# The opening of a transformer kernel: first modulation, first norm and the latents' products put into one block, and two later orders changed

## The reference, cut to what matters

```python
mod = silu(c) @ w_ada + b_ada                      # six sections of D: shift1, scale1, gate1, ...
h = rms_norm(x, norm1_g) * (1 + scale1) + shift1
z = h @ w_in                                       # 1024 x (256, 256, 64, 512, 512, 512)
c_q, c_kv, k_pe, dq, dk, dv = split(z)
q  = rms_norm(c_q, q_a_norm_g) @ w_q_up            # "latents": c_q and c_kv
kv = rms_norm(c_kv, kv_a_norm_g) @ w_kv_up
k_pe, dq, dk = rope(...)
lam = exp(sum(lambda_q1*lambda_k1)) - exp(sum(lambda_q2*lambda_k2)) + 0.2
d_out = norm((softmax(q1 k1) - lam * softmax(q2 k2)) v)
x = x + gate1 * (concat(mla_out, d_out) @ w_out)
h2 = rms_norm(x, norm2_g) * (1 + scale2) + shift2
for each block of 128 rows of one expert (32 experts, top 1 group of 4, top 2 of 8):
    y = (silu(xb @ w_gate[e]) * (xb @ w_up[e])) @ w_down[e]    # D_EXPERT = 512
x = rms_norm(x + gate2 * moe, final_norm_g)
# second block: rms_norm, modulate, conv mixer (three products D x D, ...), gated FFN
```

## Time and profile before

| | before |
|---|---|
| median of 3 runs (lowest, highest) | 2682.98 us (2680.89, 2684.83) |
| the profiled execution: its own time | 2683.05 us |
| its span | 2681.3 us |
| mean granted TensorE clock | 0.945 |
| PE busy | 2384.5 us (89%), 10764 matmuls |
| DVE busy | 1738.9 us (65%) |
| ACT busy | 1216.7 us (45%) |
| moved | 485.28 MB, mean 181 GB/s |

### The profile page before, as it was taken

How to read it: one execution, slowest core, us unless ns; L and a number is a source line. 1 busy time by engine, 2 the same in 40 slices (tenths; PEclk the granted TensorE clock), 3 DMA queues, 4 the chain that set the end, 5 groups by cost and what they waited for, 6 DMA issues and landing times. The chain is left out here.

```text
span 2681.3 us, 31591 instructions
## 1 busy us (share of the span) xinstructions
PE 2384.5 (89%) x10764; PEld 1908.4 (71%) x10764; DVE 1738.9 (65%) x1997; ACT 1216.7 (45%) x1623; POOL 450.7 (17%) x396
## 2 busy tenths in 40 slices
PE   2889996799798399999999759999899999999998
PEld 2667775477567288787777547887677888888886
DVE  5368886466495589999999665444338666653344
ACT  2236675366531277677676461110464333332332
POOL 0000000787500011000000110000004323220100
PEclk9899997899898599999999869999999999999999
DMA  5131121337655499999999863331532323245453
GB/s 207 44 118 36 48 70 39 105 97 244 231 180 194 146 390 398 398 399 398 397 399 397 300 227 104 109 110 56 172 91 67 94 70 89 75 121 185 146 171 115
DMA packets 268905, 485.28 MB, mean 181 GB/s; under 512 B 19410, under 2 KB 129423, under 8 KB 268303
## 3 DMA queue, kind: packets, MB, share of 16 engines
q1 hardware_dynamic: 235568, 364.37, 39.4%
q0 software_dynamic: 26912, 98.62, 11.1%
q10 hardware_dynamic: 6336, 21.11, 2.0%
HBM read 402.24 MB, written 76.55 MB: 179 GB/s over the span
## 5 line engine op out<-in xcount | busy, mean ns | idle before, releaser
L2059 DVE TENSOR_TENSOR e_w<-e_raw,e_w 128x1024 fp32r<-128x1024 f32 x384 | 442.2, 1217 | 60.2 <-ACT e_w L2123 59.7
L2123 ACT ACTIVATE e_w<-e_raw 128x1024 fp32r<-128x1024 f32 x384 | 376.6, 1050 | 191.4 <-PE e_pgu L255 148.1
L255 PE MATMUL e_pgu<-e_w,e_xt 128*128 128x512 f32 x1536 | 369.0, 397 | 16.5 <-DVE e_xt L2067 10.2
L255 PEld LDWEIGHTS e_pgu<-e_w,e_xt 128*128 128x128 f32 x1536 | 286.0, 189 | 91.1 <-DVE e_w L2059 17.8
L255 PE MATMUL s_ps<-h,s_w 128*128 128x512 f32 x1152 | 267.0, 394 | 5.4 <-DVE h L2459 5.4
L255 PEld LDWEIGHTS s_ps<-h,s_w 128*128 128x128 f32 x1152 | 218.9, 190 | 52.2 <-DVE h L2459 5.9
L255 PE MATMUL w_ps<-w_out,w_ring 128*128 128x512 f32 x1056 | 244.1, 390 | 2.2 <-DVE w_ring L3094 2.2
L255 PE MATMUL w_ps<-y 128*128 128x512 f32 x1056 | 240.2, 389 | 1.4 <-DVE w_o_full L3259 1.0
L255 PEld LDWEIGHTS w_ps<-w_out,w_ring 128*128 128x128 f32 x1056 | 198.1, 188 | 45.1 <-DVE w_out L3101 3.0
L255 PEld LDWEIGHTS w_ps<-y 128*128 128x128 f32 x1056 | 198.0, 188 | 43.4 <-issue 1.4
L255 PE MATMUL w_ps<-y,w_ring 128*128 128x512 f32 x816 | 195.9, 398 | 4.3 <-ACT w_h L2891 3.0
(11 more groups left out here) (388 smaller groups left out, 3882.5 us busy)
## 6 DMA issues: line engine op xcount, KB each, us to landing
e_raw<-in_w_expert_gate_dram SPq DMA_DIRECT2D x128, 512.0 KB, 6.7
e_raw<-in_w_expert_up_dram SPq DMA_DIRECT2D x128, 512.0 KB, 6.9
e_raw<-in_w_expert_down_dram SPq DMA_DIRECT2D x128, 512.0 KB, 7.1
w_raw<-in_ffn_w_gate_up_dram SPq DMA_DIRECT2D x48, 512.0 KB, 6.0
w_o_full<-in_ffn_w_down_dram SPq DMA_DIRECT2D x44, 512.0 KB, 4.0
y_rows<-am_zrow SPq DMA_DIRECT2D x4, 4352.0 KB, 34.3
raw_rows<-in_w_ada_dram POOLq DMA_DIRECT2D x32, 512.0 KB, 4.0
y_rows<-e_yo ACTq DMA_DIRECT2D x32, 512.0 KB, 6.3
```

Of the source, the lines that this page charges most:

```text
L255: o = pe.matmul(out, stat[i], mov[j], start=start and n == 0, stop=stop and n == 2)
L2059: dve.tensor_tensor(w[1][:, slot % CUT], raw[:, slot], w[0][:, slot % CUT].bitcast(F32), ALU.subtract).then_inc(low, 1)
L2123: act.activation(w[0][:, slot % CUT], raw[:, slot], ACT.Copy).then_inc(high, 1)
```

## The change

1. `load_constants`, `first_modulation` and `norm_transposed` are gone. Their work stands at the head of `diff_attention`'s block. x comes first, in eight pieces, then section 0 and section 1 of w_ada in eight pieces each through one set of eight slots. Each block of 128 rows of x is squared, scaled (now by ACT, out of `x_rows`) and turned as it comes; four of the turned blocks are copied out of PSUM by DVE (`copy_x`), four by ACT. DVE adds the sections (`add_section`) in between, the modulation is added up into columns, and `modulate(k)` (DVE, in place on `m_full`) makes h's chunk k, which is split at once.
2. The four latents are no longer made one after another. `latents()` takes the chunks k of depth in turn and does 24 matmuls for each, into eight PSUM banks, so that it begins with the first chunk of h and of the weights. The shared key (`LAT` is now 1 for the numbering of chunks) follows, with the sums of squares between its halves. The splits of weights, roots, inverses and norms behind it are written in another order.
3. In the experts' opening the row block's split stands behind two weight pieces.
4. In the combine stage SP issues the final norm's gain and then waits for the first gathered rows before it issues the conv's weights; the splits of the weights stand behind the first blocks' work, `columns` behind `scaled(3)`, `norm(3)` and two inverses ahead of it, two adds (4 and 5) and their squares behind `split(0)`.

DVE's queue from its first rows, before. `m_acc` is the sum over a section, `n_stage` the normed rows, `n_rstd` the inverse roots.

The diff, cut to its core:

```diff
-def load_constants(nc, g, a):
...
-def first_modulation(nc, g, a, room):
...
-def norm_transposed(nc, g, tag, gain, mod, out_t=None, split=None, ahead=None):
...
-    LAT = 5
+    LAT = 1
...
+        sec = nc.alloc_sbuf_tensor_at("m_sec", [P, KD, D], F32, offset=h_at[0])
+        acc = nc.alloc_sbuf_tensor_at("m_acc", [P, 2, D], F32, offset=e0_at)
...
+        lat_w = [nc.alloc_sbuf_tensor_at(f"m_lat_w{j}", [P, KD, 4 * P], F32R, offset=g.lat_at[j]) for j in range(2)]
...
+                for n in range(NT):
+                    sp.dma_start(x_rows[:, n, :], x_v[n]).then_inc(x_in[n], 16)
+                for t in range(KD):
+                    sp.dma_start(sec[:, t, :], sec_v[:, t, 0:D]).then_inc(sec_in[t], 16)
...
+                for t in range(KD):
+                    sp.wait_ge(part, t + 1)
+                    sp.dma_start(sec[:, t, :], sec_v[:, t, D:2 * D]).then_inc(sec_in[t], 16)
+                sp.dma_start(lat_raw_w[:], win[:, :, 0:4 * P]).then_inc(lat_w_in, 16)
...
+                def latents():
...
+                    for k in range(KD):
+                        pe.wait_ge(lw_low, k + 1)
+                        pe.wait_ge(h_low, k + 1)
+                        for c in range(4):
+                            for hf in range(2):
+                                to = (ps[:, c, halves[hf]] if c < 2 else pss[:, halves[hf]] if c == 2 else (pj, po)[hf][:])
+                                o = three_passes(pe, to, [v[:, k, c * P:(c + 1) * P] for v in lat_w], [v[:, k, halves[hf]] for v in h_t],
+                                                 k == 0, k == KD - 1)
+                            if k == KD - 1:
+                                o.then_inc(lproj, 1)
...
-                for c in range(LAT):
-                    latent(c)
+                pe.wait_ge(ident_in, 16)
+                for n in range(NT):
+                    turn_x(n)
+                    if n == 4:
+                        pe.wait_ge(rows_in, 16 * 9)
+                        for q in range(2):
+                            o = pe.transpose(rows_t[:, q, :], vrow[:, q, :], g.ident[:])
+                        o.then_inc(rows_turned, 1)
+                section(0)
+                section(1)
+                latents()
+                shared_latent()
+                pe.wait_ge(lat_raw, 4)
...
+                    act.activation(full[:, :, n * P:(n + 1) * P], ps[:, n % 2, :].rearrange("p (k q) -> p k q", q=P), ACT.Copy).then_inc(x_copied, 1)
...
+                square(0)
+                for n in range(NT):
+                    if n < NT - 1:
+                        square(n + 1)
+                    scale_x(n)
+                    if n >= 5:
+                        copy_x(n - 1)
+                copy_x(NT - 1)
...
+                act.wait_ge(lat_w_in, 16)
+                for k in range(KD):
+                    act.activation(lat_w[0][:, k, :], lat_raw_w[:, k, :], ACT.Copy).then_inc(lw_high, 1)
+                    act.wait_ge(affine, k + 1)
+                    act.activation(h_t[0][:, k, :], full[:, k, :], ACT.Copy).then_inc(h_high, 1)
                 w_leading(0, 0)
                 w_leading(0, 1)
-                w_leading(1, 0)
-                for c in range(4):
...
-                    w_leading(c + 1, 1)
-                    act.activation(lraw[:, c, :], ps[:, c % 2, :], ACT.Copy).then_inc(lat_raw, 1)
...
-                    act.activation(lsq[:, c, :], lraw[:, c, :], ACT.Square).then_inc(squared, 1)
-                    if c == 2:
-                        latent_root(0)
-                    if c < 3:
-                        w_leading(c + 2, 0)
...
+                latent_evict(0)
+                latent_evict(1)
+                latent_square(0)
+                latent_square(1)
+                latent_evict(2)
+                latent_evict(3)
+                latent_square(2)
+                latent_square(3)
+                w_leading(LAT, 0)
+                latent_root(0)
+                w_leading(LAT, 1)
+                latent_root(1)
                 latent_leading(0)
-                latent_root(1)
-                w_leading(LAT, 0)
-                w_leading(LAT, 1)
                 for c in range(3):
...
+                def copy_x(n):
...
+                    dve.tensor_copy(full[:, :, n * P:(n + 1) * P], ps[:, n % 2, :].rearrange("p (k q) -> p k q", q=P)).then_inc(x_copied, 1)
...
+                def modulate(k):
+                    dve.tensor_scalar(full[:, k, :], full[:, k, :], g.a_col[:, k:k + 1], g.mod[:, 0, k:k + 1], ALU.mult, ALU.add).then_inc(affine, 1)
...
+                inverse(0)
+                inverse(1)
+                copy_x(0)
+                inverse(2)
+                copy_x(1)
+                add_section(0)
+                inverse(3)
+                copy_x(2)
+                add_section(1)
+                inverse(4)
+                copy_x(3)
+                for t in range(2, 5):
+                    add_section(t)
+                    inverse(t + 3)
...
+                for t in range(5, KD):
+                    add_section(t)
+                dve.wait_ge(rows_turned, 1)
+                dve.tensor_copy(g.vcol[:], rows_t).then_inc(vec_ready, 1)
+                for t in range(KD, 2 * KD):
+                    add_section(t)
...
+                dve.tensor_tensor(g.mod[:, 0, :], pcol, g.col["first_b"], ALU.add).then_inc(mod_ready, 1)
...
+                dve.scalar_tensor_tensor(out=g.a_col[:], in0=g.mod[:, 0, 8:16], scalar=1.0, in1=g.col["norm1_g"], op0=ALU.add, op1=ALU.mult).then_inc(mod_ready, 1)
...
+                modulate(0)
+                for k in range(KD):
+                    lat_w_rest(k)
+                    if k < KD - 1:
+                        modulate(k + 1)
+                    h_rest(k)
...
+                w_rest(0)
+                w_rest_part(LAT, 0)
                 latent_inverse(0, 0)
+                w_rest_part(LAT, 1)
                 latent_inverse(0, 1)
-                w_rest_part(4, 0)
                 latent_norm(0, "q_g")
-                w_rest_part(4, 1)
+                latent_inverse(1, 0)
                 latent_rest(0)
-                w_rest_part(LAT, 0)
-                latent_inverse(1, 0)
-                w_rest_part(LAT, 1)
+                w_rest_part(LAT + 1, 0)
                 latent_inverse(1, 1)
+                w_rest_part(LAT + 1, 1)
                 latent_norm(1, "kv_g")
-                w_rest_part(LAT + 1, 0)
-                w_rest_part(LAT + 1, 1)
                 latent_rest(1)
...
-                rest_gu(0, range(CUT))
+                rest_gu(0, (0, 1))
                 x_rest(0)
-                rest_gu(0, range(CUT, 8))
+                rest_gu(0, range(2, 8))
...
+                sp.dma_start(fg[:], a["final_norm_g"].partition_broadcast(P)).then_inc(fg_in, 16)
+                sp.wait_ge(rows_in[0], 32)
                 for j, s in enumerate(order):
                     sp.dma_start(raw[:, j], w_v[:, :, s, 0:P]).then_inc(raw_in[j], 16)
-                sp.dma_start(fg[:], a["final_norm_g"].partition_broadcast(P)).then_inc(fg_in, 16)
-                sp.wait_ge(rows_in[0], 32)
...
-                for j in range(3):
-                    rest(0, j)
                 add(0)
                 add(1)
                 norm(0)
...
                 add(3)
                 norm(2)
                 inverse(1)
+                norm(3)
+                inverse(2)
+                rest(0, 0)
+                inverse(3)
+                rest(0, 1)
                 dve.wait_ge(col_out, 1)
                 dve.scalar_tensor_tensor(out=g.a_col[:], in0=g.mod2[:, 0, 8:16], scalar=1.0, in1=g.col["g0"], op0=ALU.add, op1=ALU.mult)
                 dve.tensor_copy(g.b_col[:], g.mod2[:, 0, 0:8]).then_inc(ab, 1)
-                norm(3)
-                inverse(2)
+                split(0)
+                rest(0, 2)
                 add(4)
-                inverse(3)
                 add(5)
-                split(0)
```

374 lines of the change are left out of this document (158 added, 216 removed).

## The result

| | before | changed |
|---|---|---|
| median of 4 runs (lowest, highest) | 2682.41 us (2680.89, 2684.83) | 2647.28 us (2646.87, 2647.80) |
| span of the profiled execution | 2681.34 us | 2645.66 us |

A forecast was written before the change was run, and what follows sets the result against it. PE, busy 89% of the span, was taken as the bound, with gains where it idles or waits. 2683.05 - 32.2 (opening, latents) - 5.4 (experts' start) - 0 (combine's start) = 2645.4 us; range 2634 to 2658.

The forecast's parts named there:

- A: Opening and latents up to the first scores: scores at 162.9 instead of 195.14, a gain of 32.2 us.
- B: Experts' start: x's split behind two weight pieces, not six, gains 5.4 us; bounds 0 and -5.6.
- C: Combine stage's start: earlier first add, given back by late acc and deferred adds, total 0; bounds -8 and +4.
- first root's end: Latents: ACT's first root, queued behind a weights' split that waits for PE, ends at 112.7; before, at 128.8.
- the start at the low clock: Latents' first products: PE's start at the low clock level adds 3 us to the 43.5 of 192 products.
- The rival of a slower DVE: Opening: copies cost 2.46 and modulates 1.28, first product 4.9 + 1.0 later, total 2651.3 to 2653; chance 0.17.
- w_in's load: Opening: w_in's 2 MB land at 42, hidden behind DVE's section adds.
- the room as some 9: Experts: a piece asked for 18.45 us ahead, less 6.8 landing and 2.3 split, leaves some 9 to spare.
- The rival in which the loads set the pace: Experts: loads set the pace after all, so the earlier start gains 0, total 2650.8; chance 0.08.
- the two things that give it back: Combine: acc lands by 1566, so columns at about 1573; two adds (5.2) and squares (3.1) deferred behind the split.
- the landing near 1558: Combine: by the skill's page small rows get a larger share, acc lands by about 1558, the stage gains 7.
- the rival of a low clock: Latents: PE fed by chunks stays at the low clock, each of 240 products 0.227 longer, total 2697; chance 0.03.

The follow-up runs named there:

- copies_act: The changed kernel, but all eight turned blocks of x are copied by ACT, none by DVE: 2643.98 us, ratio 0.9856.
- whole_h: The changed kernel, but PE begins the latents' products only when all eight chunks of h and of the weights are split: 2662.12 us, ratio 0.9924.
- root_first: The changed kernel, but the first latent root precedes the next weights' leading part on ACT, and its inverse that chunk's rest on DVE: 2642.74 us, ratio 0.9855.
- load_after: The changed kernel with one more 2 MB transfer, read by nobody, on SP's queue ahead of the experts' loop: 2652.02 us, ratio 0.9883.
- adds_early: The changed kernel, but the combine stage's adds 4 and 5 and their squares stand ahead of the wait for columns: 2644.26 us, ratio 0.9858.
- acc_first: The changed kernel, but the two stored sections are issued ahead of the conv's weights, whose second and third splits stand behind affine and split: 2640.69 us, ratio 0.9845.

## Why the prediction was right

The steps came mostly as laid out. That the total lies within 1.9 owes something to luck: A fell short by 1.0, B and C gave 0.7 and 0.4 more, and the stretches that the change does not touch added 2.0, which nobody forecast.

- **The opening.** Its steps, forecast and found: last section add 43.7 and 45.0; first product 51.4 and 52.49; last of 192 products 97.9 and 98.0; first root's end 112.7 and 112.92; scores 162.9 and 163.86. The agreement at 98.0 is two errors that cancel: the first product came 1.1 late, and the products took 45.6 and not 46.5, as the start at the low clock cost 2.0 and not 3. That DVE bounds the front was tested by taking its copies away (copies_act, -3.9), that PE sets the pace behind it by withholding the chunks (whole_h, +17.1 for 16.4 of delay), and that DVE's chain bounds most of the rest by moving the root (root_first, -3.0 for 4.3).
- **Mis-sized there.** DVE's section adds ended 1.3 late, because its copies and inverses reached it later than I laid out (the last root was out at 29.5 and not at 28.0; section 0's last add ended at 34.3, not 33.2, with the copy of the columns only behind it), and because the seven adds of section 1 took 1.37 each and not 1.31. Copy and modulate cost 1.23 and 0.81, where I took 1.21 and 0.75. The rival of a slower DVE did not come.
- **w_in's load** landed at 45.5, not at 42: I had the sections' last pieces arriving without a gap, but two of them waited for DVE's adds. It did not show in the time, as the modulation came later still; the cover was 3 us and not 6.
- **B.** -5.7 at the first product and -6.1 at the last split, where I took -5.4; undoing it alone cost 5.6 in the stage. The reason given, PE setting the pace because ACT hardly waits for landings, was half of the truth. The transfers stand level with PE: with 116 us of PE's work gone they still ran at 399 GB/s, and the stage was 1.7 shorter. What let PE gain 5.7 was the lead of at least 5.1 that each piece had. I counted the room as some 9, of which 5.6 go; the closest pieces had 5.1, and are now split 0.1 to 0.7 behind their landing. The rival in which the loads set the pace was nearer than its 0.08 said: in load_after a transfer that its expectation puts at about 5.3 us cost 4.7, so by that estimate some 0.6 was left.
- **C.** The place of the two things that give it back was right, and so was their size: moved by the 34.9 between the two last expert products, acc landed at 1565.8 (forecast 1566), `columns` came at 1572.9 (1573), the first product at 1583.3 (1583.5), and the second half's last scaling ended at 1604.9 (1606.5: what was deferred took 21.7 and not 23.0). adds_early and acc_first each took one of the two away and got 2.7 and 6.7.
- **The share of the rows of 512 B.** The count of one small row for one big one holds where both stand ready: from 1514 to 1518 us of the changed kernel the gathers' queue (q0) and SP's (q1), with the weights' small rows, moved 371 packets each:

```profile
q0 software_dynamic: 371, 1.37, 87.8%
q1 hardware_dynamic: 371, 0.19, 16.3%
```

  But the gathers did not run without a pause, as I had it; in the pauses the small rows went faster (602 packets of q1 beside 112 of q0 from 1512 to 1514), and the gathers ended near 1565 and not 1559 (moved as above). The third piece of weights landed at 1563.3 and not 1562, and the sections behind it took 2.5 and not 4: that acc came within 0.2 is in part luck. The Trainium skill (DMA: Bandwidth & Descriptors, Queues, rings and completion order) says that an engine drains a whole packet of several descriptors from one queue before it changes to the next. That section does not say whether a turn takes more small rows than large ones, so the landing near 1558 was a reading put on it, and it is this reading that the 371 against 371 do not bear out.
- **The clock.** While PE was fed chunk by chunk it was granted 0.89 (50 to 79 us) where it had 0.73 in the earlier trace rows, and 1.00 from 60 to 70, while DVE still made chunks, and from 70 to 76; the rival of a low clock did not come:

```profile
50.00:79.00 29.00, 26.51 (x109) 21.85 (x110) 19.68 (x26) 12.65 (x17) 0.00 (x0) 0.89 0.18 47
60.00:70.00 10.00, 10.00 (x46) 8.27 (x45) 8.92 (x12) 4.44 (x6) 0.00 (x0) 1.00 0.00 0
70.00:76.00 6.00, 6.00 (x28) 4.99 (x27) 0.76 (x2) 0.72 (x2) 0.00 (x0) 1.00 0.74 187
```

## What to carry to other kernels

Few waits for a transfer do not mean that transfers have room: read the time from issue to landing as well, and take from it the lead that is left; a gain at such a stage's start is paid out of that lead once. When small and large rows share the engines, issue first what the next stage's chain needs, not what is needed in bulk. A step that is deferred past a split should go into an existing wait of its engine, provided that the short operation which ends the wait does not stand behind it.

## What the runs showed of the hardware

- One core drew 398 to 399 GB/s for hundreds of microseconds, and 512 KB in 1.28 in the opening (410 GB/s). The Trainium skill (DMA: Bandwidth & Descriptors, Where 436 GB/s comes from) gives some 358 GB/s for each of the two cores that share an HBM stack and says that this side binds loads from HBM; with one core at work it did not bind here.
- A table load on ACT took 1.28 and the next activation began 0.02 behind it (9.85 to 11.15). The Trainium skill (ScalarE: Activation LUTs, What ACT_TABLE_LOAD costs) adds 1.38 of draining; here none is seen, neither behind the load nor ahead of it (ACT's instruction before it ended at 9.84).
- A reciprocal of 128 x 512 on DVE took 3.35, an add, copy or subtraction of twice the elements 1.2 to 1.3. The four reciprocals are 13.4 of the 51 us between the first root and the scores.
- Rows of 512 B and rows of 4 KB in two queues went one for one where both stood ready (371 packets each in 4 us), so the small rows got 0.19 MB beside 1.37.
